# A mixer in three token blocks, two of them worked off between the slots of an expert gather

## What is computed

```python
proj = x @ w_in                      # 2048 columns: lru_x 512, gate 512, sc_B, sc_C, sc_x, mem_q 256 each
y_lru = rg_lru(conv4(lru_x)) * gelu(gate)          # gates by 64x64 blocks, a scan along the tokens
y_sc  = sc_B * conv3(sc_C * sc_x)
y_mem = softmax(q @ mem_k.T / 8) @ mem_v           # 4 heads, 256 memory tokens
x1 = layernorm(alpha * x + concat(rmsnorm(y_lru), rmsnorm(y_sc), rmsnorm(y_mem)) @ w_out)
q  = x1 @ wq                                       # 8 heads x 2 sides x 128
e, g = product_keys_top16(q, keys)                 # 16 experts of 16384 per token and head, and their gates
f  = sum_k g[k] * gelu(x1 . u[e[k]]) * v[e[k]]
y  = layernorm(alpha * x1 + f)
```

## Time and profile before

| | us |
|---|---|
| runs of the kernel | 3402.91, 3400.89, 3385.37, median 3400.89 |
| the profiled execution | 3404.87 |
| its span | 3403.0 |
| PE busy | 2607.5 (77%) |
| DVE busy | 2134.4 (63%) |
| ACT busy | 1320.1 (39%) |
| POOL busy | 1151.2 (34%) |
| first gather issued | 554.84 |
| mean granted clock of PE | 0.799 |

### The profile page before, as it was taken

How to read it: one execution, slowest core, us unless ns; L and a number is a source line. 1 busy time by engine, 2 the same in 40 slices (tenths; PEclk the granted TensorE clock), 3 DMA queues, 4 the chain that set the end, 5 groups by cost and what they waited for, 6 DMA issues and landing times.

```text
span 3403.0 us, 37868 instructions
## 1 busy us (share of the span) xinstructions
PE 2607.5 (77%) x11476; PEld 944.3 (28%) x11476; DVE 2134.4 (63%) x4722; ACT 1320.1 (39%) x3873; POOL 1151.2 (34%) x1092
## 2 busy tenths in 40 slices
PE   8989898888777767767777777777677778866766
PEld 4665444233322222222222221222122224410010
DVE  1453646778866676667666766676666665565454
ACT  1432102554444444444444444344434433343343
POOL 0000002444443444444444444443444443343342
PEclk9989998878877787887777777778877776677677
DMA  5001155999999999999999999999999997899998
GB/s 191 19 19 74 63 198 226 421 398 408 415 421 421 421 404 422 416 412 409 421 419 404 414 416 421 421 405 416 421 405 413 418 421 303 319 421 421 421 421 333
DMA packets 175261, 1209.03 MB, mean 355 GB/s; under 512 B 19792, under 2 KB 23120, under 8 KB 34768
## 3 DMA queue, kind: packets, MB, share of 16 engines
q0 software_dynamic: 156672, 1140.92, 81.5%
q1 hardware_dynamic: 18384, 65.68, 5.2%
HBM read 1192.02 MB, written 14.51 MB: 355 GB/s over the span
## 4 chain that ended last, share of the span: by engine, by line
issue 41%; POOL 25%; PE 20%; DMA 6%; DVE 5%; ACT 2%; POOLq 0%; SPq 0%; DVEq 0%; ACTq 0%
POOL arena L444 25%; PE ps L481 7%; DMA arena<-in_uv,idxT 6%; PE ps L620 4%; PE ps L721 3%; DVE arena L1327 2%; PE ps L655 2%; PE ps L705 1%; PE ps L670 1%; PE ps L497 0%; PE ps L525 0%; PE ps L459 0%; PE ps L536 0%; POOLq L442 0%; PE ps L515 0%
## 5 line engine op out<-in xcount | busy, mean ns | idle before, releaser
L721 PE MATMUL ps<-arena,wset 128*32 128x512 f32 x4352 | 1460.5, 798 | 695.2 <-ACT wset L955 622.7
L444 POOL DMA_INDIRECT arena<-in_uv,idxT x1088 | 1151.0, 1058 | 2223.7 <-PE ps L721 1580.5
L1327 DVE CUSTOM_DVE_ANT_0 arena<-arena 128x1024 f32<-128x1024 f32 x1088 | 1331.2, 1225 | 911.0 <-DMA arena<-in_uv,idxT 843.9
L946 ACT ACTIVATE gel<-acts 128x1 f32<-128x1 f32 x1088 | 219.8, 202 | 1395.3 <-DVE acts L1327 1382.5
L721 PEld LDWEIGHTS ps<-arena,wset 128*32 128x32 f32 x4352 | 187.9, 123 | 1735.1 <-ACT wset L955 1512.1
L955 ACT ACTIVATE wset<-arena,wt 128x32 f32<-128x32 f32 x1088 | 349.5, 321 | 54.2 <-PE ps L721 18.4
L950 ACT ACTIVATE wt<-gel,gT 128x1 f32<-128x1 f32 x1088 | 320.4, 294 | 103.1 <-ACT gel L946 3.4
L655 PEld LDWEIGHTS ps<-arena 128*128 128x128 f32 x2304 | 315.2, 220 | 124.5 <-issue 124.5
L655 PE MATMUL ps<-arena 128*128 128x128 f32 (+1 forms) x2304 | 340.4, 310 | 0.7 <-issue 0.7
L705 PE MATMUL ps<-arena 32*128 32x512 f32 x704 | 265.7, 839 | 5.3 <-ACT arena L925 3.8
L481 PE MATMUL ps<-arena 128*128 128x384 f32 (+1 forms) x768 | 247.4, 481 | 0.7 <-ACT arena L835 0.7
(11 more groups left out here) (154 smaller groups left out, 1408.6 us busy)
## 6 DMA issues: line engine op xcount, KB each, us to landing
arena<-in_uv,idxT POOLq DMA_INDIRECT x1088
arena<-in_w_in SPq DMA_DIRECT2D x16, 512.0 KB, 3.5
arena<-in_x_tok SPq DMA_DIRECT2D x9, 512.0 KB, 4.8
scratch_x<-arena SPq DMA_DIRECT2D x9, 512.0 KB, 3.0
scratch_x1T<-arena SPq DMA_DIRECT2D x9, 512.0 KB, 2.6
arena<-scratch_x1T SPq DMA_DIRECT2D x9, 512.0 KB, 4.3
arena<-in_w_out SPq DMA_DIRECT2D x1, 4096.0 KB, 13.2
arena<-in_xT SPq DMA_DIRECT2D x2, 1536.0 KB, 13.8
```

Of the source, the lines that this page charges most:

```text
L444: pool.indirect_dma_start(out=ring[n % RING], out_offset=None, in_=A["uv"], in_offset=bass.IndirectOffsetOnAxis(ap=idxT[t % 2][:, col:col ...
L721: last = mm(ps[r0:r0 + 32, hf * HALF:(hf + 1) * HALF], wset[n % SETS][:, :], v[:, hf * HALF:(hf + 1) * HALF], start=first, stop=final)
L946: A_(gel[:, n % COLS:n % COLS + 1], acts[:, n % COLS:n % COLS + 1], ACT.Gelu).then_inc(gelus, 1)
L1327: V.tensor_tensor_reduce(out=ring[n % RING][:, 0:D], in0=ring[n % RING][:, 0:D], in1=xrep[g % 2], scale=1.0, scalar=0.0, op0=ALU.mult, op1 ...
```

## The change

Every stage of the mixer now works on one block of tokens, and there are three: 384, 384, and 256 prompt tokens with the 64 of the samples. What a block leaves for the next (three columns per convolution, the scan's state) is kept in small tiles. Each stage has a name, and a plan says for each of PE, ACT, DVE and SP at which step it stands; each engine's entries are sorted by step. Steps below 0 come before the slots, steps from 0 on are the slots' numbers.

Block 0 lies wholly before slot 0 up to the routing of the first unit. The rest of its layernorms and queries are in steps 0 to 74, block 1 starts at step 76, block 2 at 384, and the last query of block 2 is at 663. In each step n an engine first calls `mix(n)`, which runs what the plan has up to n, and then does the slot's own work. Stages are generators: a pace says how many pieces go into one step.

Further parts: one semaphore per engine (`stage`) and a count per stage replaces the separate ones. Weight tiles of 512 KB (input projection, output projection of blocks 1 and 2, query weights, the sample caches) stream through three buffers, for every block anew, in the plan's order. The queries no longer stand in the slots' windows; they are computed per block (128 tokens of it first, for tile 0), stored to memory (`sq`), and loaded for each unit in rows of 2 KB (`load_q`). The turned x1 is no longer stored and reloaded. Tile 3's units have windows of 16 slots instead of 32. The first layernorm is one pass over the tile shorter. The ring now lies in space of its own; its first four buffers hold the memory projection's inputs before, the next the output weights.

```diff
+BLOCKS = [(0, 384, 384, 3), (384, 384, 384, 3), (768, 256, 320, 3)]
+LEAD = -200
+BASE = [LEAD, 76, 384]
...
+def plan_later_block(b):
...
+    o = BASE[b]
+    put("sp", o - 6, b, "xT")
+    for i, (name, c) in enumerate(PROJ):
+        put("pe", o + 8 * i, b, "half", (name, c))
+        put("pe", o + 8 * i + 4, b, name, c)
+        put("act", o + 8 * i + 6, b, name, c)
+    for c in range(CL):
+        x = o + 16 * c
+        put("dve", x + 25, b, "cv", c)
+        put("pe", x + 31, b, "gr", c)
+        put("act", x + 31, b, "sr", c)
+        put("pe", x + 31.5, b, "gi", c)
+        put("act", x + 32, b, "si", c)
+        put("act", x + 33, b, "ta", c)
+        put("dve", x + 34, b, "ra", c)
+        put("act", x + 39, b, "sd", c)
+        put("dve", x + 40, b, "re", c)
...
+def plan_queries(b, x, each):
...
+    for side in range(SIDES):
+        put("pe", x + each * side, b, "wq", side)
+        put("act", x + each * (side + 1), b, "we", side)
+        if side % 4 == 3:
+            put("sp", x + each * (side + 1) + 1, b, "sq", side // 4)
...
+PE_PACE = {"half": 0.5, "oq": 1, "wq": 0.5, "w0": 0.25, "xt": 0.25, "nm": 0.25, "ss": 0.25, "sv": 0.25}
...
+def stepper(entries, run, pace):
...
+    state = [0, None, 0.0]
...
+    def advance(n):
+        while True:
+            if state[1] is None:
+                if state[0] == len(entries) or entries[state[0]][0] > n:
+                    return
+                s, b, name, arg = entries[state[0]]
+                state[1], state[2] = run(b, name, arg), max(s, n)
+            if state[2] > n:
+                return
+            if next(state[1], "end") == "end":
+                state[0], state[1] = state[0] + 1, None
+            elif n >= 0:
+                state[2] += pace(*entries[state[0]][1:3])
...
+    def after(eng, who, b, name, arg=0):
...
+        eng.wait_ge(stage[who], DONE[who][(b, name, arg)])
...
+        mix = stepper(PLAN["pe"], run, lambda b, name: 0.33 if (b, name) == (0, "wq") else PE_PACE.get(name, 0))
+        for v in range(LEAD, 0):
+            mix(v)
...
         for n in range(NSLOT):
+            mix(n)
             g, i = SLOT[n][4:6]
             if i == 0 and g + 1 < len(GROUPS_OF):
                 replicate(g + 1)
             if n in AT:
                 u = AT[n]
                 keyscores(u)
...
```

More of the change, by code:

```diff
@@ new lines, with put @@
+W_COL.update({("sb", i): 2 * CL + i for i in range(CS)})
+W_COL.update({("sC", i): 2 * CL + CS + i for i in range(CS)})
+W_COL.update({("sx", i): 2 * CL + 2 * CS + i for i in range(CS)})
+W_COL.update({("qp", i): 2 * CL + 3 * CS + i for i in range(CM)})
+GROUPS = [(2, [6, 7], D_MEM), (0, [0, 1, 2, 3], D_LRU), (1, [4, 5], D_SC)]
+ROUNDS = [6, 6, 4]
+G_MEM, G_LRU, G_SC = 0, 1, 2
+PLAN = {"pe": [], "act": [], "dve": [], "sp": []}
+def put(eng, step, b, name, arg=0):
+    PLAN[eng].append((step, b, name, arg))
@@ new lines @@
+plan_first_block()
+plan_later_block(1)
+plan_later_block(2)
+for _e in ("pe", "act", "dve"):
+    PLAN[_e].sort(key=lambda x: x[0])
+STREAMED = {"oq", "wq", "w0", "ss", "sv"} | {n for n, _ in PROJ}
+_began = {(b, *a): s for s, b, n, a in PLAN["pe"] if n == "half"}
+W_USE = sorted([(_began.get((b, n, a), s), b, n, a) for s, b, n, a in PLAN["pe"] if n in STREAMED],
+               key=lambda x: x[0])
+for _i in range(len(W_USE)):
+    PLAN["sp"].append((LEAD - 1 if _i < WIN else W_USE[_i - WIN + 1][0], W_USE[_i][1], "win", _i))
@@ L181, in build @@
[L181 to L186, removed]
-    xt, x1o, x1To = [None, None], [None, None], [None, None]
-    xt[1], x1o[1], x1To[1], xt[0], x1o[0], x1To[0] = (n.take(D) for _ in range(6))
-    rep0 = c.take(D)
-    sel = c.take(4 * P + 4 * 32)
+    TM = 392
+    a = Carver(sb("arena", [P, 50552])[:, :], 0)
+    ring = [a.take(2 * D) for _ in range(RING)]
@@ new lines, in _ @@
+        for n in range(NSLOT):
+            mix(n)
+            if n in q_at:
+                load_q(q_at[n])
+            if n == 20:
+                load_x1(1)
+            t = SLOT[n][0]
+            if n in x1_at:
+                sp.wait_ge(res_done, x1_at[n] - 1)
+                load_x1(x1_at[n])
+            if t >= 1 and n - TILE_END[t - 1] == FINISH + 8:
+                sp.wait_ge(yo_ready, t)
+                store_y(t - 1)
+        after(sp, "dve", 2, "sh", CS - 1)
+        sp.dma_start(O["states"], st[:, :]).then_inc(st_state, 16)
@@ new lines, in claim, with landed, project @@
+        def claim(k, who, b, name, arg=0):
+            if k in holder:
+                after(pe, *holder[k])
+            holder[k] = (who, b, name, arg)
+            return bank[k]
+        def landed(b, name, arg):
+            i = W_AT[(b, name, arg)]
+            pe.wait_ge(ld_win[i % WIN], 16 * (i // WIN + 1))
+            return win[i % WIN]
+        def project(b, name, c, k0, k1, out_):
+            w_ = landed(b, name, c).rearrange("p (k m) -> p k m", k=KD)
+            x_ = x8(zone1, b)
+            for kk in range(k0, k1):
+                last = mm(out_, w_[:, kk, :], x_[:, kk, :], start=kk == 0, stop=kk == KD - 1)
+                if kk == KD - 1:
+                    last.then_inc(stage["pe"], 1)
+                yield
@@ L1313, in finish @@
             yield
-        for _ in route(0):
-            pass
-        copy_idx(0)
-        layernorm1(NL - 1)
+        mix = stepper(PLAN["dve"], run, lambda b, name: DVE_PACE.get(name, 0.5))
+        for v in range(LEAD, 0):
+            mix(v)
         u, pieces, closing = 0, iter(()), iter(())
         for n in range(NSLOT):
+            mix(n)
             t, c_, m_, h, g, i = SLOT[n]
```

1529 lines of the change are left out of this document (840 added, 689 removed).

## The result

| | before | after |
|---|---|---|
| median of the runs | 3393.13 us (4 runs) | 3273.99 us (4 runs, 3267.31 to 3280.60) |
| the profiled execution, its span | 3404.87, 3403.0 us | 3267.31, 3265.3 us |
| PE, DVE, ACT, POOL busy | 77, 63, 39, 34% | 77, 66, 44, 37% |
| first gather | 554.84 us | 211.47 us |
| bytes moved | 1209.03 MB | 1265.55 MB |

The changed kernel takes 0.965 of the time before (95% interval 0.961 to 0.969), 3.5% less. Predicted were 3260 us and, for the profiled execution, 3266. The kernel before lands either near 3383 or near 3402 us (27 and 15 of 42 executions, none between) and its profiled one is of the second kind, while the change's is the fastest of its four: so the profiles lie 137.7 us apart, the medians 119, and predicted were 139 and 141.

A forecast was written before the change was run, and what follows sets the result against it. DMA gathers bound the slots, after a first part with DMA nearly idle. 3404.9 - 326 - 45 + 152 + 65 + 15 = 3266, less 4 to the median, rounded: 3260 us; range 3195 to 3360.

The forecast's parts named there:

- The start of the gathers: Before the slots: with only block 0 computed first, the first gather goes out at 229 us instead of 555, gaining 326 us.
- a chain of 11: End of block 0's mixer: last short convolution, squares, root, reciprocal and norm in one chain, some 11 us.
- the 20 us for stages that wait for each other: Block 0 before the slots: fewer columns cover waits between stages less, 10 to 40 us added, 20 taken.
- The weights and blocks, 152 us: In the slots: 67.9 MB of added weight tiles and block traffic displace their own bytes, net 152 us lost.
- rival D: In the slots: the added traffic is hidden anyway, 3040 us; chance 0.03.
- The queries' traffic, 65 us: In the slots: storing and reloading queries, 15.7 MB in 2 KB rows, costs 38 to 91 us, 65 taken.
- The lag, 15 us: Mixed steps: the ring absorbs hold-ups under some 12 us; unhidden rest 0 to 60 us, 15 lost taken.
- The sample tile's dip, 45 us: Sample tile, 2683 to 3223 us before: its queries leave the slots and the lost DMA rate returns, gaining 45 us.
- Compute stays hidden: Mixed steps 0 to 667: DMA needs 2.90 us a step, PE 2.08 to 2.63, DVE 2.05, ACT 1.5.
- rival A: Steps with projections or queries: PE at 1.2 GHz becomes the bound, 3.96 us a step, some 3500 us; chance 0.12.
- Rival B: Mixed steps: late stages delay slots beyond the ring's slack, 1 to 1.5 us per table step, 3320 to 3350; chance 0.15.
- C: Before the slots: block 0's chain runs serially, first gather near 320 to 350 us, total 3350 to 3385; chance 0.10.

## Why the prediction came out

**The start of the gathers: right, 17 us too cautious.** Timeline of the changed kernel:

```profile
154.65 22.24 PE L817 MATMUL ps<-arena 128*128 128x512 f32 x48 [6.10 <-DVEq L1187]
...
178.55 3.81 PE L859 MATMUL ps<-arena 128*128 128x128 f32 x32 [0.79 <-DVEq L1187]
```

```profile
211.47 1.07 POOL L671 DMA_INDIRECT arena<-in_uv,idxT  x1 [211.02 <-DVE idxT L1472]
```

The output projection starts at 154.65 us; predicted were 163 and a chain of 11, 174. From there to the queries it is 23.9 us (predicted 13.7 + 6.5 + 3), from the queries to the gather 32.9 (predicted 32). The mis-sized term is the 20 us for stages that wait for each other: PE's waits for ACT are 8.1 us at L698 and 2.4 at L806, and its wait for DVE before the output projection is 6.1 of the chain's 11; what makes up the rest of the 19 us isn't split. In the other runs the start is 212.3 to 218.5 us, so 10 to 17 us is what this term is off by.

**The weights and blocks, 152 us: right.** The bytes came out as counted (1265.55 MB against "near 1265"), and these loads cost about their bytes: 2.06 us per MB in the run with half the weights, for 2.4 taken. By that a seventh of the weights' price is hidden, on average; all of it (rival D) is excluded.

**The queries' traffic, 65 us: the step that failed.** The prediction took "the nearest row", the dip at the x1 load, as the price of a 2 KB row: 5.8 us per MB as a bound, 4.1 as the value. What it read there is real, for an x1 load costs 4.0 to 5.8 us per MB wherever it stands, but it isn't a price of the rows' length: query loads in the same rows cost 2.45, and over their stores the rate stays at 420 GB/s. So the 15.7 MB cost some 38 us. The stores' half of this rests on such windows, no run prices stores alone.

**The lag, 15 us: too small.** That the ring catches any hold-up under 12 us was an estimate and doesn't hold: in the run with later x1 loads, with no such load beside it, a wait of PE of 3.43 us, and 5.9 and 5.3 us between three gathers instead of 2.49 each, went with 3.9 us of missing bytes. It isn't always so: the wait of 6.08 us in the kernel before left the DMA share at 1.01. Losses against 421 GB/s outside the sample tile were 53 us before (98 - 45) and are 115 now, so the lag is 62. Some 45 of it are in the two stretches (50, less 5 that as many quiet us lose). 14 us are shown to be three buffers for four uses in a row. In the other stretch VectorE's own work accounts for 9.5, its waits for ScalarE likely for some 3 to 8; what the rest of its 27 us hangs on stays open. The errors cancel: 27 too much for the queries' rows and 17 too little gain at the start against 47 too little for the lag. The sum of 3266 for a measured 3267.31 is better than its terms, and in part it is luck of the pair: by the medians the gain is 119 us for 141 predicted. In which term these 20 us are can't be read, for there is one profile of each kernel.

**The sample tile's dip, 45 us: gone as predicted.** From 2150 us to the end no slice but the last is below 410 GB/s; the earlier trace rows had 386 in its whole stretch.

**Compute stays hidden: right.** The mixed steps are 2.91 us (655 dot products in 1909 us) for 2.90 predicted, a tile 373 for 370, the last tiles 326 (2.55 us a slot, by the gathers of slot 704 at 2258 us and of slot 1087 at 3234.1) for 325. The clock in the mixed part is 0.81 to 0.93, and 0.73 behind it, where PE is busy 67% and not 82% of the time. The denser part has the higher clock, as the page "TensorE: Matmul & The Clock Gate" of the Trainium skill, section "What's actually happening", has it (though not the 20 us of the earlier trace rows, fully busy at 0.50), and rival A, in which denser steps would be granted 1.2 GHz, did not come. The table loads rose from 114 to 194 over all lines, 80 more where some 110 were expected, among others because a tanh needs none. The largest group, ahead of the slots' gelus, had 42 before:

```profile
L1127 ACT ACT_TABLE_LOAD x80 | 102.6, 1283 | 6.4 <-DVE acts L1526 5.0
```

Rival B had 57 to 86 us of waits, one at each table step; the lag of 62 is of that size, but bunched in two places and not at those steps, so that its waits came in the amount of B and the rows' overprice paid for them. C is excluded by 211.47.

## What to carry to other kernels

A ledger of three numbers (when the full stretch begins, its bytes at the full rate, what it loses against that rate) tells in a few rows whether an overlap pays, and where a sum is right only by luck. A phase that leaves the DMA engines idle is worth moving under one that fills them, even if the move makes it read its weights three times: 744 us of work went under gathers for 281 us. When the rate dips beside a transfer, look at the DMA share before giving a price: a share that falls with the rate is a wait, and every engine's timeline says whose; a share that stays full means that the bytes on the engines took longer. Here both lay in one place, and only moving the transfer parted them. And a price found for one transfer isn't that of every transfer with rows of the same length. In a plan written by hand, uses in a row must not outnumber the buffers.

## What was unexpected of the hardware

Query loads in 2 KB rows beside a full stream of 8 KB gathers cost no more than their bytes (2.45 us per MB over 25.2 MB, with 421 GB/s as the full rate), while x1 loads with rows of the same length pull the rate down to 355 GB/s and lower at a DMA share of 1.02, wherever they stand; why stays open. And Tanh runs without a table load both behind Gelu and behind Sigmoid, while Sigmoid, Exp and Sqrt between gelus cost a load of 1.28 us each way.
